# Two multiplications by one over the sums placed behind score steps, and GpSimd's weight residues computed in two halves

## The chip, the cores and the metric

One core of one Trainium2 chip runs the whole program as one launch. The metric is the device time of that launch in microseconds (us); the time before is the median of three runs. A profile of one further execution goes with it. Engines are named as in the profile: PE is TensorE (PEld its weight loads), DVE is VectorE, ACT is ScalarE, POOL is GpSimd, SP is the queue that issues most of the loads.

## The reference, cut to what matters

Two transformer-like blocks in float32 on a sequence of 1024 tokens of width 1024. The first block is gated linear attention with a short convolution and a feed-forward layer; the second is a spatial gating branch beside a dilated attention with 16 heads of 64. The part that the change touches is the dilated attention and every dense product with a weight matrix:

```python
s = einsum('bhrnqd,bhrnkd->bhrnqk', qb, kw) * Dh ** -0.5 - slopes * dist * dilation
p = exp(s - max(s)); l = sum(p)
o = einsum('bhrnqk,bhrnkd->bhrnqd', p, vw) / l
```

The kernel computes the three dilation patterns as one causal attention with a bias (distance times slope plus the logarithm of how many patterns hold the pair), which gives the same mixture.

## The kernel before, in words

**Dense products.** All weights are cut into 197 units of 1024 x 128. float32 accuracy is made from three reduced-precision products: high part of the weight by high part of the input, high by low, low by high (L791 to L793, and L974 to L976 in a part that works on sums of blocks). One unit is 16 groups of these three matmuls with 512 columns. For each unit SP loads the raw weights (`w_raw`, 128 x 1024), ACT copies them to the high part (`w_hi`, L1185), and POOL subtracts to get the low part, the residue (`w_lo`, L686). Two slots are used in turn. SP's next load into a slot waits for the residue's semaphore `w_lo` of that slot's unit, and PE's unit begins with a wait for `w_hi` and `w_lo`. The feed-forward and projection parts that use block sums have their own residue code (L721), in pieces of 128 x 512.

**Attention.** It runs under 32 further dense units: 8 pairs of heads, and for each pair four stages m = 0, 1, 2, 3 (head m // 2, token half m % 2). I call m = 0 and 2 early stages, m = 1 and 3 late stages. Into the 16 dense groups of a stage's unit PE weaves small steps, and each engine has a hand-written order of steps (`PE_STEPS`, `ACT_STEPS`, `DVE_STEPS`, one string for early and one for late stages). A stage works on its own scores and at the same time finishes the stage before it. The steps are:

- `s` on PE (L1094, L1095): a chunk of scores into PSUM (`aux`). Late stages have eight, s0 to s7, for four token blocks with two chunks each. s(n) waits until `r(n-2)` is done, because two PSUM banks alternate.
- `r` on DVE (L2215): adds the bias, keeps the row minimum, writes to the buffer of p (`att_p_late` or `att_p_early`); it is followed by a short read of the accumulator.
- `e` on ACT (L1595): the exponential of a token block with its row sum.
- `n` on DVE (L2225 and L2227, function `normed`): one over the row sum, then the multiplication of the block of p by it. In late stages the blocks are 640, 768, 896 and 1024 wide. PE's first transposition of the next stage waits for all four.
- `t` on PE (L1110): transposes p of the stage before; `p` on ACT (L1605): its high part; `l` on DVE (L2234, `p_lo`): its low part; `o` on PE (L1122, L1123): multiplies by v. `o(k)` waits for `l(k)`, and `t(k)` for `l(k-1)`.
- `z` on DVE (L2198) copies the unit's result out of PSUM; `w` on ACT is the high part of the next unit's weights, after which POOL makes the residue; `m` (L2250) finishes a gate and is there only in m = 1 (for the stage before, m - 1 = 0) and in m = 2; `b` (L2091), `q` (L2096), `k` (L2101) prepare the next head; `O` adds the two halves of the output; `v` splits v and is there only in m = 1.

In stage m = 1 POOL multiplies y by its gate first (L756), then makes the residue (L686), and after `m` multiplies another tile (L751). In m = 3 it has only the residue.

An engine works its own list strictly in order: whatever stands behind a waiting step waits as well.

Of the kernel before, what the change touches and what calls it, by code (L numbers as in the profile page):

```python
# [106 lines left out]
def group(q):  # L107

    return q - 6 if 6 <= q < 14 else None
# [61 lines left out]
def chunks_of(m):  # L171
# [25 lines left out]
]  # L197
DVE_STEPS = [
    "O l0 k l1 z l2 r0 l3 r1 n0 l4 r2 n1 l5 r3 n2 l6 m n3 l7",
    "v0 r0 v1 O r1 r2 z n0 l0 r3 r4 n1 l1 r5 m r6 r7 l2 n2 b l3 n3 q",  # L200
]

PE_REST = "t0 t1//o0 t2//o1 t3//o2 t4//o3 t5//o4 t6//o5 t7//o6//o7//".split("/")
# [26 lines left out]
def two_blocks(nc, xT, weights, vecs, gate_up, mix_w, mix_b, dist, logm, ident, out):  # L230
    f32, f32r = mybir.dt.float32, mybir.dt.float32r
    ALU = mybir.AluOpType
# [3 lines left out]
    with ctx:  # L236
# [4 lines left out]
        def place(name, cols, dt=f32, offset=None, rows=P):  # L241
            nonlocal top
            shape = [rows] + (list(cols) if isinstance(cols, (list, tuple)) else [cols])
            size = 4 * int(np.prod(shape[1:]))
            if offset is None:
                offset, top = top, top + (size + 63) // 64 * 64
            at[name] = offset
            return nc.alloc_sbuf_tensor_at(name, shape, dt, offset=offset)
# [6 lines left out]
        WR = place("w_raw", [2, KT, P])  # L255
        WH = place("w_hi", [2, KT, P], f32r)
        WL = place("w_lo", [2, KT, P], f32r)
# [83 lines left out]
        def sem(name):  # L341
            return ctx.enter_context(nc.semaphore(name))
# [5 lines left out]
        w_hi, w_lo, mm_done, evac = sem("w_hi"), sem("w_lo"), sem("mm_done"), sem("evac")  # L348
# [51 lines left out]
        def product(p, i, six, pair):  # L400

            return (six, 6 * p + i + 1) if i < 6 else (pair, units_before(p) + 2)
# [8 lines left out]
        def half(p, i):  # L411
            return (7 * own(p) + i + 2 + (min(p // 4, 3) if p < DUOS else min(own(p) // 8, 1))) % 4
# [15 lines left out]
        def quarter(p, i):  # L428

            if i in (0, 1, 3, 6):  # L430
                return WS[:, (0, 1, 3, 6).index(i)]
            row, col = {2: (0, 0), 4: (0, 1), 5: (1, 1)}[i]
            return w_pair(p)[:, row].rearrange("p (j e) c -> p e j c", e=2)[:, col]
# [23 lines left out]
        def all_stages(engine, stage):  # L457


            first, final = Pair(0), Pair(PAIRS - 1)  # L460
            stage(first, 0, head=False)
            stage(first, 1, before=(first, 0))
            with engine.Fori(0, PAIRS - 1) as j:
                now, following = Pair(0, j), Pair(1, j)
                stage(now, 2, before=(now, 1), done=(now, 0))
                stage(now, 3, before=(now, 2), done=(now, 1))
                stage(following, 0, before=(now, 3), done=(now, 2))
                stage(following, 1, before=(following, 0), done=(now, 3))
            stage(final, 2, before=(final, 1), done=(final, 0))
            stage(final, 3, before=(final, 2), done=(final, 1), head=False)  # L470
# [211 lines left out]
        @block.gpsimd  # L682
        def _(pool):
            def split(u):
                pool.wait_ge(w_hi, u.count(1))
                pool.tensor_tensor(WL[:, u.slot], WR[:, u.slot], WH[:, u.slot].bitcast(f32),  # L686
                                   ALU.subtract).then_inc(w_lo, 1)

            def splits(c, n):
                if n >= 2:  # L690
                    with pool.Fori(0, n // 2) as i:
                        split(Unit(c, i, 2))
                        split(Unit(c + 1, i, 2))
                if n % 2:
                    split(Unit(c + n - 1))

            pool.memset(ONES[:], 1.0).then_inc(consts, 1)
            for u in range(2, U_OUT + 2):
                split(Unit(u))
                if u == 3:  # L700
                    pool.wait_ge(rs, 1)
                    pool.memset(RESET, 1.0).then_inc(g_const, 1)
                    pool.wait_ge(g_const, 1)
                    pool.memset(RESET.rearrange("p (c t) -> p c t", t=CHUNK)[:, :, 0:1], 0.0).then_inc(g_const, 1)
                if u == 10:
                    pool.wait_ge(g_tp, 4)
                    for s in range(2):
                        pool.memset(SC[:, s], 0.0).then_inc(g_const, 1)
                if u - 2 in AT_SCORES:
                    for h in (2 * AT_SCORES.index(u - 2), 2 * AT_SCORES.index(u - 2) + 1):  # L710
                        pool.wait_ge(sc_cp, h + 1)
                        pool.affine_select(out=SC[:, h % 2], in_=SC[:, h % 2], compare_op=ALU.is_ge, fill=0.0,
                                           base=0, pattern=[[0, NBLK], [1, P]], channel_multiplier=-1
                                           ).then_inc(sc_sel, 1)
            splits(U_OUT + 2, U_DUO - U_OUT - 2)

            def lo_half(p, i):
                pool.wait_ge(*product(p, i, d_hi, w_hi))
                h = half(p, i)
                at4 = slice(4 * (h % 2), 4 * (h % 2) + 4)  # L720
                pool.tensor_tensor(WL[:, h // 2, at4], quarter(p, i), WH[:, h // 2, at4].bitcast(f32),  # L721
                                   ALU.subtract).then_inc(*((d_lo, 1) if i < 6 else (w_lo, 2)))

            for p in range(DUOS):
                for i in range(7):
                    lo_half(p, i)
            splits(U_DOWN, V_DUO - U_DOWN)

            def mask(g):
                pool.wait_ge(gat_in[g % 2], 32 * (g // 2 + 1))  # L730
                w3 = MIXES[:, g % 2, 0:1]
                pool.affine_select(out=w3, in_=w3, compare_op=ALU.is_ge, fill=0.0, base=0,
                                   pattern=[[0, 1], [1, P]], channel_multiplier=-1).then_inc(w_sel, 1)

            for q in range(V_DUOS):
                for i in range(7):
                    lo_half(DUOS + q, i)
                    if i == 2 and group(q) is not None:
                        mask(group(q))
            splits(U_ATT, 2)  # L740


            def stage(pair, m, before=None, done=None, head=True):
                if m == 1 and done:
                    gate_y(done[0])
                if before:
                    split(pair.unit(m).plus(1))
                if m == 1:
                    pool.wait_ge(gated, pair.count(2, 1))
                    pool.wait_ge(mx_in, pair.count(16, 16))  # L750
                    pool.tensor_tensor(MXL[:], MXL[:], AG[:], ALU.mult).then_inc(ya_up, 1)  # L751

            def gate_y(pair):
                pool.wait_ge(yh, pair.count(4, 4))
                pool.wait_ge(gated, pair.count(2, 2))
                pool.tensor_tensor(Y[:], Y[:], SBG[:], ALU.mult).then_inc(yb_up, 1)  # L756

            all_stages(pool, stage)
            split(Unit(U_PA + 1))
            gate_y(Pair(PAIRS - 1))  # L760
            splits(U_PA + 2, UNITS - U_PA - 2)
            for t in range(2):
                pool.wait_ge(rs, 6 + t)
                for k in ENDED_BY_ACT:
                    dst = XR[:, k, t * HALF:(t + 1) * HALF]
                    pool.tensor_tensor(dst, dst, R[:, t * HALF:(t + 1) * HALF], ALU.mult).then_inc(fin_pool, 1)
# [1656 lines left out]
```

## Time and profile before

| | us |
|---|---|
| median of three runs | 2412.66 |
| lowest and highest of the runs | 2410.06, 2413.32 |
| the profiled execution's own time | 2410.62 |
| its span in the profile | 2408.9 |
| PE busy | 2351.6 (98% of the span) |
| DVE busy | 1345.0 (56%) |
| ACT busy | 861.6 (36%) |
| POOL busy | 736.6 (31%) |

The mean granted clock of PE over the span is 0.994 of full speed. Spans on PE are modelled: a 512-column matmul is shown as 0.39 us long, while in an undisturbed stretch the next one starts 0.23 us after it. So what a wait costs is read from starts, not from ends. The attention lies between about 1523 and 2118 us of the span.

### The profile page before, as it was taken

How to read it: one execution, taken by the hardware profiler on the slowest of the kernel's cores; microseconds unless marked ns; L12 is line 12 of the kernel's file. 1: busy time of each engine (PE TensorE's matmuls, PEld its weight loads, DVE VectorE, ACT ScalarE, POOL GpSimd, SP SyncE). 2: the span in 40 equal slices, each digit the busy share in tenths (PEclk: the TensorE clock that was granted, in tenths of full speed). 3: DMA queues.
4: the chain of work that ended last, by engine and by line, in shares of the span. 5: the costliest groups of instructions: out<-in, count | busy, mean ns of one | idle time of the engine just before them, and what ended most of it. 6: DMA issues, size and time to landing. Idle time of an engine off the chain costs nothing.

```text
span 2408.9 us, 29740 instructions
## 1 busy us (share of the span) xinstructions
PE 2351.6 (98%) x11076; PEld 1938.9 (80%) x11076; DVE 1345.0 (56%) x1790; ACT 861.6 (36%) x1293; POOL 736.6 (31%) x416
## 2 busy tenths in 40 slices
PE   9999999999999999999999999999999999999997
PEld 6888788878888888888888888778787787778886
DVE  4444763754444443347653444777877778753444
ACT  4422222242333331143343223555545555441122
POOL 2121221264555522222455555211122112212221
PEclk9999999999999999999999999999999999999998
DMA  3111222232222243233312223523233232353223
GB/s 133 44 44 35 88 79 96 86 144 85 79 79 80 84 169 105 70 114 114 118 53 83 101 95 111 178 76 113 78 113 106 77 113 78 105 181 124 105 96 113
DMA packets 69168, 237.94 MB, mean 99 GB/s; under 512 B 8241, under 2 KB 10449, under 8 KB 68945
## 3 DMA queue, kind: packets, MB, share of 16 engines
q1 hardware_dynamic: 53568, 181.53, 22.2%
q10 hardware_dynamic: 15504, 55.10, 5.7%
q8 instruction: 65, 1.06, 0.2%
q14 instruction: 31, 0.25, 0.0%
HBM read 177.35 MB, written 59.24 MB: 98 GB/s over the span
## 4 chain that ended last, share of the span: by engine, by line
PE 93%; DVE 4%; issue 1%; DMA 1%; ACT 1%; SPq 0%; DVEq 0%; ACTq 0%
PE dense L791 18%; PE dense L792 18%; PE dense L793 18%; PE dense L974 9%; PE dense L975 9%; PE dense L976 9%; PE aux L1110 3%; PE aux L1094 2%; PE aux L1095 1%; PE aux L1123 1%; PE aux L1122 1%; PE aux L1057 1%; DVE att_p_lo L2234 1%; DVE x_lo L1964 1%; PE aux L821 0%
## 5 line engine op out<-in xcount | busy, mean ns | idle before, releaser
L686 POOL TENSOR_TENSOR w_lo<-w_raw,w_hi 128x1024 fp32r<-128x1024 f32 x123 | 303.3, 2466 | 1097.0 <-ACT w_hi L1185 1087.9
L791 PE MATMUL dense<-x_hi,w_hi 128*128 128x512 f32 x1456 | 596.7, 410 | 5.8 <-DVE x_lo L1736 2.1
L792 PE MATMUL dense<-x_lo,w_hi 128*128 128x512 f32 x1456 | 570.7, 392 | 0.0
L793 PE MATMUL dense<-x_hi,w_lo 128*128 128x512 f32 x1456 | 570.7, 392 | 0.0
L1185 ACT CAST w_hi<-w_raw 128x1024 fp32r<-128x1024 f32 x121 | 127.1, 1050 | 555.7 <-PE dense L793 548.8
L793 PEld LDWEIGHTS dense<-x_hi,w_lo 128*128 128x128 f32 x1456 | 274.8, 189 | 59.8
L791 PEld LDWEIGHTS dense<-x_hi,w_hi 128*128 128x128 f32 x1456 | 275.5, 189 | 56.6 <-issue 8.6
L792 PEld LDWEIGHTS dense<-x_lo,w_hi 128*128 128x128 f32 x1456 | 276.1, 190 | 46.6 <-issue 1.9
L721 POOL TENSOR_TENSOR w_lo<-w_sums,w_hi 128x512 fp32r<-128x512 f32 x144 | 228.3, 1594 | 240.9 <-ACT w_hi L1341 240.9
L974 PE MATMUL dense<-x_hi,w_hi 128*128 128x512 f32 x576 | 226.1, 392 | 0.0
L976 PE MATMUL dense<-x_hi,w_lo 128*128 128x512 f32 x576 | 224.2, 389 | 0.0
L975 PE MATMUL dense<-x_lo,w_hi 128*128 128x512 f32 x576 | 224.2, 389 | 0.0
L1341 ACT CAST w_hi<-w_sums 128x512 fp32r<-128x512 f32 x144 | 89.2, 620 | 242.8 <-DVE w_sums L1973 176.1
L974 PE MATMUL dense<-x_sums_split,w_hi 128*128 128x512 f32 x432 | 168.4, 390 | 2.4 <-DVE work L2180 1.2
L976 PE MATMUL dense<-x_sums_split,w_lo 128*128 128x512 f32 x432 | 168.2, 389 | 0.0
L975 PE MATMUL dense<-x_sums_split,w_hi 128*128 128x512 f32 x432 | 168.1, 389 | 0.0
L1605 ACT CAST att_p_hi<-aux 128x512 fp32r<-128x512 f32 x192 | 92.2, 480 | 145.9 <-PE aux L1110 145.5
L2234 DVE TENSOR_TENSOR att_p_lo<-aux,att_p_hi 128x512 fp32r<-128x512 f32 x192 | 106.3, 554 | 60.3 <-ACT att_p_hi L1605 58.0
L791 PE MATMUL dense<-work_split,w_hi 128*128 128x512 f32 x352 | 137.0, 389 | 1.5 <-DVE work L2049 1.5
L793 PE MATMUL dense<-work_split,w_lo 128*128 128x512 f32 x352 | 136.9, 389 | 0.0
L792 PE MATMUL dense<-work_split,w_hi 128*128 128x512 f32 x352 | 136.9, 389 | 0.0
L974 PEld LDWEIGHTS dense<-x_hi,w_hi 128*128 128x128 f32 x576 | 108.2, 188 | 23.0 <-issue 1.0
(270 smaller groups left out, 3815.7 us busy)
## 6 DMA issues: line engine op xcount, KB each, us to landing
w_raw<-weights SPq DMA_DIRECT2D x163, 512.0 KB, 4.1
w_raw_b<-weights SPq DMA_DIRECT2D x34, 512.0 KB, 4.3
kept_qkv<-work ACTq DMA_DIRECT2D x24, 512.0 KB, 2.7
kept_m<-work ACTq DMA_DIRECT2D x22, 512.0 KB, 2.6
work<-kept_m SPq DMA_DIRECT2D x22, 512.0 KB, 3.3
residual<-xT SPq DMA_DIRECT2D x16, 512.0 KB, 7.1
kept_x<-residual ACTq DMA_DIRECT2D x16, 512.0 KB, 2.6
att_q<-kept_qkv SPq DMA_DIRECT2D x32, 256.0 KB, 3.9
```

The costliest lines, as they stand in the source:

```text
L686: pool.tensor_tensor(WL[:, u.slot], WR[:, u.slot], WH[:, u.slot].bitcast(f32), ALU.subtract).then_inc(w_lo, 1)
L721: pool.tensor_tensor(WL[:, h // 2, at4], quarter(p, i), WH[:, h // 2, at4].bitcast(f32), ALU.subtract).then_inc(*((d_lo, 1) if i < 6 else ...
L791: pe.matmul(dst, WH[:, u.slot, k], hi, start=(k == 0), stop=False)
L792: pe.matmul(dst, WH[:, u.slot, k], lo, start=False, stop=False)
L793: last = pe.matmul(dst, WL[:, u.slot, k], hi, start=False, stop=(k == nk - 1))
L974: pe.matmul(bank(b), wh, hi[:, j], start=(first and j == 0), stop=False, skip_group_check=True)
L975: pe.matmul(bank(b), wh, lo[:, j], start=False, stop=False, skip_group_check=True)
L976: last = pe.matmul(bank(b), wl, hi[:, j], start=False, stop=(j == 3), skip_group_check=True)
L1185: act.copy(WH[:, u.slot], WR[:, u.slot]).then_inc(w_hi, 1)
L1341: act.copy(WH[:, h // 2, 4 * (h % 2):4 * (h % 2) + 4], quarter(p, i)).then_inc(*((d_hi, 1) if i < 6 else (w_hi, 2)))
L1605: act.copy(PH[:, k % 2, lo:HALF], PA[:, bank, lo:HALF]).then_inc(ph, 1)
L2234: dve.tensor_tensor(PL[:, k % 2, lo:HALF], PA[:, bank, lo:HALF], PH[:, k % 2, lo:HALF].bitcast(f32), ALU.subtract).then_inc(pl, 1)
```

## The change

In late stages the multiplication of the first block, n0, moves from behind `z` to behind `r4`, so that `l0`, `r3` and `r4` come before it. The second, n1, moves from behind `r4` to behind `r5`, so that `l1` and `r5` come before it. Early stages stay as they are. The residue of a unit is made by two POOL instructions of 128 x 512 in place of one of 128 x 1024; the semaphore is incremented by the second one alone. That holds for every unit whose residue `split` makes, throughout the kernel, 123 by the profile.

```diff
 DVE_STEPS = [
     "O l0 k l1 z l2 r0 l3 r1 n0 l4 r2 n1 l5 r3 n2 l6 m n3 l7",
-    "v0 r0 v1 O r1 r2 z n0 l0 r3 r4 n1 l1 r5 m r6 r7 l2 n2 b l3 n3 q",
+    "v0 r0 v1 O r1 r2 z l0 r3 r4 n0 l1 r5 n1 m r6 r7 l2 n2 b l3 n3 q",
 ]
...
             def split(u):
                 pool.wait_ge(w_hi, u.count(1))
-                pool.tensor_tensor(WL[:, u.slot], WR[:, u.slot], WH[:, u.slot].bitcast(f32),
-                                   ALU.subtract).then_inc(w_lo, 1)
+                for at4 in (slice(0, 4), slice(4, 8)):
+                    last = pool.tensor_tensor(WL[:, u.slot, at4], WR[:, u.slot, at4],
+                                              WH[:, u.slot, at4].bitcast(f32), ALU.subtract)
+                last.then_inc(w_lo, 1)
```

## Rows read from the trace of the kernel before

**Rows 1.** Who waited for whom on PE, all of the span: total, times, longest (us)
```profile
PE aux L1094 <- DVE softmax_stats L2215: 25.1, 16, 1.9
PE aux L938 <- ACT work L1287: 3.3, 1, 3.3
```
**Rows 2.** PE in order of time, stages m = 1 (1696) and m = 3 (1733): start, length
```profile
1693.92 0.39 PE L793 MATMUL dense<-x_hi,w_lo 128*128 128x512 f32 x1
1696.22 0.45 PE L1094 MATMUL aux<-att_k_hi,att_q_split 128*128 128x384 f32 x1 [1.91 <-DVE softmax_stats L2215]
1696.50 0.34 PE L1095 MATMUL aux<-att_k_lo,att_q_split 128*128 128x384 f32 x1
1696.68 0.40 PE L1122 MATMUL aux<-att_p_hi,att_v_split 128*128 128x512 f32 x1
...
1733.21 0.44 PE L1094 MATMUL aux<-att_k_hi,att_q_split 128*128 128x384 f32 x1 [1.24 <-DVE softmax_stats L2215]
```
**Rows 3.** DVE in order of time in the stage m = 1 at 1696
```profile
1692.37 0.15 DVE L2225 RECIPROCAL softmax_stats<-softmax_stats 128x1 f32<-128x1 f32 x1
1692.56 2.61 DVE L2227 TENSOR_SCALAR att_p_late<-att_p_late,softmax_stats 128x640 f32<-128x640 f32 x1
1695.09 0.68 DVE L2234 TENSOR_TENSOR att_p_lo<-aux,att_p_hi 128x512 fp32r<-128x512 f32 x1
1695.69 0.47 DVE L2215 CUSTOM_DVE_ANT_0 att_p_late<-aux,att_bias,softmax_stats 128x256 f32<-128x256 f32 x1
...
1697.46 0.62 DVE L2227 TENSOR_SCALAR att_p_late<-att_p_late,softmax_stats 128x768 f32<-128x768 f32 x1
...
1704.59 0.28 DVE L2234 TENSOR_TENSOR att_p_lo<-aux,att_p_hi 128x128 fp32r<-128x128 f32 x1
```
**Rows 4.** ACT and POOL in order of time in the same stage
```profile
1692.22 0.59 ACT L1605 CAST att_p_hi<-aux 128x512 fp32r<-128x512 f32 x1
1697.69 0.48 ACT L1605 CAST att_p_hi<-aux 128x384 fp32r<-128x384 f32 x1 [0.46 <-PE aux L1110]
1692.42 2.39 POOL L686 TENSOR_TENSOR w_lo<-w_raw,w_hi 128x1024 fp32r<-128x1024 f32 x1
```
**Rows 5.** POOL and DVE in order of time in an early stage, m = 2
```profile
1635.20 2.40 POOL L686 TENSOR_TENSOR w_lo<-w_raw,w_hi 128x1024 fp32r<-128x1024 f32 x1 [7.54 <-ACT w_hi L1185]
...
1636.59 0.68 DVE L2234 TENSOR_TENSOR att_p_lo<-aux,att_p_hi 128x512 fp32r<-128x512 f32 x1
```
**Rows 6.** Waits from 1523 to 2118 (one row), then PE's timeline in the stage m = 1
```profile
PEld aux L1122 <- DVE att_p_lo L2234: 2.0, 6, 0.4
...
1704.60 0.40 PE L793 MATMUL dense<-x_hi,w_lo 128*128 128x512 f32 x1
1704.93 0.33 PE L1122 MATMUL aux<-att_p_hi,att_v_split 128*128 128x128 f32 x1
...
1705.60 0.49 PE L791 MATMUL dense<-x_hi,w_hi 128*128 128x512 f32 x1 [0.23 <-issue]
```
**Rows 7.** Busy time by window (after POOL: granted clock, DMA share, GB/s), then PE's timeline
```profile
1620.40:1624.40 4.00, 4.00 (x13) 3.27 (x14) 2.85 (x8) 2.83 (x5) 0.00 (x0) 0.58 0.00 0
...
1620.36 0.44 PE L1094 MATMUL aux<-att_k_hi,att_q_split 128*128 128x384 f32 x1 [1.91 <-DVE softmax_stats L2215]
1658.32 0.44 PE L1094 MATMUL aux<-att_k_hi,att_q_split 128*128 128x384 f32 x1 [1.24 <-DVE softmax_stats L2215]
```
**Rows 8.** Groups by line and shape on POOL (busy us, mean ns), then one row of its timeline
```profile
L686 POOL TENSOR_TENSOR w_lo<-w_raw,w_hi 128x1024 fp32r<-128x1024 f32 x123 | 303.3, 2466 | 1097.0 <-ACT w_hi L1185 1087.9 <-ACT w_hi L1582 4.5 <-ACT w_hi L1421 4.5
...
512.31 1.29 POOL L721 TENSOR_TENSOR w_lo<-w_raw_b,w_hi 128x512 fp32r<-128x512 f32 x1
```
**Rows 9.** DVE in order of time in the convolution, before the wait at L938
```profile
282.45 3.28 DVE L1906 TENSOR_TENSOR work<-work,rstd 128x1024 f32<-128x1024 f32 x1
```
**Rows 10.** POOL and PE in order of time where the first attention unit begins
```profile
1518.32 2.58 POOL L686 TENSOR_TENSOR w_lo<-w_raw,w_hi 128x1024 fp32r<-128x1024 f32 x1 [4.53 <-ACT w_hi L1582]
...
1522.72 0.47 PE L791 MATMUL dense<-x_hi,w_hi 128*128 128x512 f32 x1 [0.62 <-DVE work L2180]
```

## The prediction

> **What bounds the kernel now.** The table has PE busy for 98% of the span, so PE's stream sets the end and only its waits can be won. I read the waits of PE first: the largest by far is that of the score matmul for DVE's running minimum, 25.1 us in 16 times; the next is 3.3 us, once [rows 1]. There are 16 late stages, so it is one wait in each. PE's timeline shows where: at the 384-column chunk, which is s5, 1.91 us in a stage m = 1 and 1.24 us in a stage m = 3 [rows 2]; 8 x 1.91 + 8 x 1.24 = 25.2 us. s5 waits for r3.
>
> DVE's timeline shows why r3 is late. n0's multiplication, of 640 columns, takes 2.61 us, while n1's, of 768, takes 0.62 us [rows 3]. POOL's residue runs from 1692.42 to 1694.81 [rows 4], and n0 ends 0.36 us behind its end: n0 stood still beside POOL and then ran in some 0.56 us. l0 and r3 stood behind it on DVE. The high part that l0 needs was there at 1692.81 [rows 4].
>
> **What a wait costs in PE's stream.** Undisturbed, a 512-column matmul is followed by the next after 0.23 us, so s5 would have started at 1693.92 + 0.23 = 1694.15; it started at 1696.22, 2.07 us late [rows 2]. Its successor comes after 0.28 us where the next step takes 0.18 us [rows 2], 0.10 us more. So m = 1 loses 2.17 us, and m = 3, by the same 0.26 us on top of the wait, 1.50 us.
>
> **Part 1, n0 behind r4.** From 1692.37, where n0's reciprocal began, DVE now waits for the high part and runs l0 from 1692.84 (0.68 us; successive DVE rows overlap by 0.08 us), then r3 from 1693.44 to about 1693.95 with the reading of its minimum [rows 3, 4]. s5 wants to start at 1694.15 and its weight load some 0.2 us earlier, so r3 is there at the last moment; in m = 3 it has 0.7 us to spare by the shorter wait (1.91 - 1.24). I count no wait at s5 and keep 0.3 us per stage m = 1 for the range. n0 then starts near 1694.7 and meets the end of POOL's second half at most; its cost lies in DVE's idle time before l1, which waits for PE's t1 and ACT's copy.
>
> **Part 2, n1 behind r5.** Before, n1 ended at 1698.08 and the high part for l1 came at 1698.17 [rows 3, 4]: n1 was in the shadow of that wait. Now it stands behind l1 and r5, with 0.15 + 0.62 us and the gap between, less one overlap, about 0.74 us, on DVE's path from t1 to the end of the stage. s6 and s7 are not reached by it, since r4 and r5 are done before. What is late next is l3. The wait of o3's weight load for l3 is there already, 6 times, 2.0 us together [rows 6]. By starts: o3 would have begun at 1704.60 + 0.23 = 1704.83 and began at 1704.93, and the dense matmul behind its two short ones came at 1705.60 [rows 6] where some 0.17 us after o3 are usual: 0.6 us lost. So in a stage m = 1 l3 sets the time of everything behind it. Before, l3 ended 1704.87 - 1698.17 = 6.70 us behind the copy that l1 waits for [rows 3, 4]; that copy comes 2.17 us earlier, the chain is 0.74 us longer, and the stage wins 2.17 - 0.74 = **1.43 us**, with a wait of l3's of about 1.1 us in its place at o3. In m = 3 there is neither `m` nor POOL's second multiplication in DVE's chain, and no such wait is in the trace; n1's 0.74 us goes into that slack and the whole **1.50 us** is won.
>
> **The clock.** In two of the eight stages m = 1 the granted clock fell behind the wait; the window 1620.40 to 1624.40 has a mean of 0.58 [rows 7], so most of it passed at 1.2 GHz, not 2.4. The price: from one restart of s5 to the next is 1658.32 - 1620.36 = 37.96 us with the fall [rows 7] and 1733.21 - 1696.22 = 36.99 us without [rows 2], 0.97 us. No stage m = 3, with 1.24 us of waiting, had one. With waits of about 1 us or less I take both away: **1.9 us**.
>
> **Part 3, the residue in halves.** POOL's instruction of 1024 columns takes 2.39 us alone, one of 512 takes 1.29 us [rows 4, 8]: 0.19 us more for each of the 123, 23 us on an engine that is busy for 31%. The group's idle time before its instructions, 1097.0 us [rows 8], is the cover. Behind POOL wait PE's next unit and SP's load. The tightest place that I looked at is the first attention unit: the residue ends at 1520.90 and PE starts at 1522.72 [rows 10], 1.8 us of slack. So 0 us. Can the halves win anything by themselves? In attention hardly, as n0 has been moved out of their way. Elsewhere a DVE instruction caught by POOL could go in between; the one case on PE's path is L1906, 3.28 us [rows 9], longer than a whole residue of 2.39 us [rows 4] and so mostly waiting. But its successors, too, work on buffers outside PSUM and would meet the second half. Bounds: +0.5 us (the second dispatch) and -1.3 us (one half less to wait for); I take 0, since POOL's time in DVE's way stays the same.
>
> **The sum.** 8 x 1.43 + 8 x 1.50 + 1.9 + 0 = 11.4 + 12.0 + 1.9 = 25.3 us. Against the profiled execution's own 2410.62 us this is 2385.3. That execution lies 2.0 us below the median of the runs, 2412.66, and the forecast is for the median: **2387.4 us**.
>
> **A rule on GpSimd and VectorE.** l0 and r3 now run while POOL makes the residue, so it matters whether they stand still as n0 did. In the early stage, where l2 fell wholly within POOL's 1635.20 to 1637.60, it took its usual 0.68 us [rows 5]; its input comes from PSUM and one SBUF buffer, as with r3. The Trainium skill, GPSIMD Engine Reference, section Key points, says that GpSimd contends with DVE instructions that run in a two-port mode or have two SBUF inputs. By that rule neither l0 nor r3 is held, and n0 and the successors of L1906 are. The trace agrees for l with 0.68 us, and no row shows a 256-column r3 beside POOL. What it would be if they were held is the second rival.
>
> **The rivals.**
> 1. *n1 finds room* (12%). If l3 were not the bound of m = 1, because the n2, `b` and l3 part shortens once POOL's multiplication falls elsewhere, each such stage would win 2.17 us and the 0.6 us at o3 in the six stages too: 8 x 2.17 + 12.0 + 1.9 + 3.6 = 34.9 us at most; with the wait at o3 unchanged 31.3 us, **2381.4 us**. Against it: n2, `b` and l3 all follow r7, which follows n1 and `m`.
> 2. *l0 and r3 are held as well*, each until POOL is done (4%): r3 would end as late as before, both moves win nothing, **2412 us**, no change. Against it speaks the 0.68 us [rows 5].
> 3. *l0 becomes the wait* (16%). DVE has nothing to do before the high part comes, and r3 and r4 queue behind l0. That part is made by ACT behind the copy of the next weights. Were it 0.5 us later than in this trace in all m = 1 stages, s5 would wait for 0.5 us or more with a restart, some 0.6 us each: 25.3 - 4.8 = 20.5; were it 1.2 us, 8 x (2.17 - 1.3 - 0.74) + 12.0 + 1.9 = 15 us, **2397.7 us**. For it: r3 is ready at the last moment as it is.
> 4. *The residue is late* (2%), the one that ends slower. POOL's two halves let DVE in between; if the residue then ended past the start of its unit, PE would wait in every unit. It decides once 1.8 us is used up [rows 10]. By 0.19 us, plus one DVE operation as long as a half, 1.29 us [rows 8], it comes to 1.5 us, so the place would hold; a further operation in between would break it, and at a loss of 0.8 us in each of 123 units the time would be 2387.4 + 98 = **2486 us**.
> 5. *The change doesn't do what it says* hardly applies: both edits are read off the code. The smallest version, in which a late r5 at s7 or another unseen wait eats half of the gain (6%), is 2400 us.
>
> **How the numbers follow.** The forecast has 60%, the rivals 12, 4, 16, 2 and 6%. The range reaches from rival 1 to rival 3, 2380.5 to 2397.5 us, which leaves out rivals 2, 4, 5 and the far end of 3. About 0.2%, 4.8 us, is what a measurement of this kernel can tell from no change, so faster means under 2407.8 us: the forecast and rivals 1, 3 and 5, 94%; the same 4%; slower 2%.
>
> **What the changed profile would show.** The row L1094 waiting for L2215, 25.1 us, is gone or below 3 us. The 640-column multiplication takes 0.56 to 0.9 us in place of 2.61 us. The weight load at L1122 waits for L2234 in all eight stages m = 1, for about 1 us each. POOL has twice the instructions at L686, of about 1.29 us, and its busy time rises by some 23 us. From s5 of an m = 1 stage to s5 of the next m = 3 stage it is still about 36.3 to 37 us without a fall of the clock, and the attention as a whole is 25 us shorter. I would be wrong if s5 still waits for 1 us or more in m = 1, if the wait at o3 stays at 0.4 us, or if PE waits for POOL anywhere.

## The result and the profile after

| | before | after |
|---|---|---|
| median, us | 2412.99 (4 runs) | 2385.43 (4 runs) |
| lowest and highest, us | 2410.06, 2414.69 | 2382.76, 2388.25 |
| the profiled execution's own time, us | 2410.62 | 2388.25 |
| its span, us | 2408.9 | 2386.5 |

The ratio of the times is 0.9887 (95% interval 0.987 to 0.9904), so the kernel is 27.6 us faster by the medians. The forecast was 2387.4 us with a range of 2380.5 to 2397.5. In the changed kernel all line numbers behind the edit are two higher and those of `split` one: the scores are L1096 and L1097, the transpositions L1112, `o` L1124 and L1125, `r` L2217, `n` L2227 and L2229, `l` L2236, the dense matmuls L793 to L795, the residue L687.

The busy times of the whole profiled execution, then the group of the residue:

```profile
PE 2350.5 (98%) x11076; PEld 1939.1 (81%) x11076; DVE 1284.5 (54%) x1790; ACT 860.8 (36%) x1293; POOL 800.7 (34%) x539
...
L687 POOL TENSOR_TENSOR w_lo<-w_raw,w_hi 128x512 fp32r<-128x512 f32 x246 | 367.7, 1516 | 1029.2 <-ACT w_hi L1187 1020.2
```

PE is the bound as before. DVE is busy 60.5 us less and POOL 64.1 us more. The waits on PE of the changed kernel, the two largest:

```profile
PE aux L1124 <- DVE att_p_lo L2236: 3.8, 8, 0.5
PE aux L940 <- ACT work L1289: 3.1, 1, 3.1
```

The row that stood first [rows 1], the scores waiting for `r3` 16 times, has no counterpart. In its place `o3` waits for `l3`, once in each of the eight stages m = 1. The wait in the convolution went from 3.3 to 3.1 us. Now the stage m = 1 that answers to [rows 2 to 4]. DVE in order of time:

```profile
1688.22 0.69 DVE L2236 TENSOR_TENSOR att_p_lo<-aux,att_p_hi 128x512 fp32r<-128x512 f32 x1 [0.38 <-ACT att_p_hi L1607]
1688.83 0.47 DVE L2217 CUSTOM_DVE_ANT_0 att_p_late<-aux,att_bias,softmax_stats 128x256 f32<-128x256 f32 x1
...
1690.04 0.68 DVE L2229 TENSOR_SCALAR att_p_late<-att_p_late,softmax_stats 128x640 f32<-128x640 f32 x1
1691.39 0.56 DVE L2236 TENSOR_TENSOR att_p_lo<-aux,att_p_hi 128x384 fp32r<-128x384 f32 x1 [0.67 <-ACT att_p_hi L1607]
...
1692.59 0.62 DVE L2229 TENSOR_SCALAR att_p_late<-att_p_late,softmax_stats 128x768 f32<-128x768 f32 x1
...
1698.53 0.28 DVE L2236 TENSOR_TENSOR att_p_lo<-aux,att_p_hi 128x128 fp32r<-128x128 f32 x1
```

ACT and POOL in the same stage:

```profile
1690.88 0.48 ACT L1607 CAST att_p_hi<-aux 128x384 fp32r<-128x384 f32 x1 [0.50 <-PE aux L1112]
...
1687.82 2.55 POOL L687 TENSOR_TENSOR w_lo<-w_raw,w_hi 128x512 fp32r<-128x512 f32 x2
```

PE in the same stage, at s5 and at o3:

```profile
1689.31 0.39 PE L795 MATMUL dense<-x_hi,w_lo 128*128 128x512 f32 x1
1689.54 0.34 PE L1096 MATMUL aux<-att_k_hi,att_q_split 128*128 128x384 f32 x1
...
1697.99 0.40 PE L795 MATMUL dense<-x_hi,w_lo 128*128 128x512 f32 x1
1698.86 0.33 PE L1124 MATMUL aux<-att_p_hi,att_v_split 128*128 128x128 f32 x1 [0.47 <-DVE att_p_lo L2236]
1699.02 0.28 PE L1125 MATMUL aux<-att_p_lo,att_v_split 128*128 128x128 f32 x1
1699.53 0.49 PE L793 MATMUL dense<-x_hi,w_hi 128*128 128x512 f32 x1 [0.23 <-issue]
```

**Read them in this order.** `l0` and `r3` ran inside POOL's 1687.82 to 1690.37 at 0.69 and 0.47 us, as long as before, so they were not held. (The 2.55 us are both halves of the residue, merged into one row.) s5 started 0.23 us behind the dense matmul before it: no wait is left. n0 began at 1690.04, 0.33 us ahead of POOL's end, and took 0.68 us in place of 2.61 [rows 3]. Then the price: n1, now behind `r5`, lies between the copy that `l1` waits for (end 1691.36) and `l3` (end 1698.81), 7.45 us in place of 6.70. o3 would have begun at 1697.99 + 0.23 = 1698.22 and began at 1698.86, and the dense matmul behind it followed after 0.67 us where some 0.17 us are usual. So PE lost 0.64 + 0.50 = 1.14 us at o3, of which the row of waits names 0.47.

**Where the time came from.** The starts of the 384-column score matmuls give it without any modelled end. The first of them is s2 of the first early stage, the last is s5 of the last stage m = 3; between them lie 2108.25 - 1529.62 = 578.63 us before and 2085.01 - 1531.72 = 553.29 us after: **25.3 us** are won inside the attention. From s5 of m = 3 to s5 of the next m = 1 it is 35.72 us after and 37.89 before (2.17 less, the term of s5 in m = 1). From s5 of m = 1 to s5 of m = 3 it is 36.19 after and 36.99 before where the clock did not fall. That is 0.80 less, where the forecast's 1.50 - 0.74 is 0.76. Together 2.97 us for each pair of stages. Outside these two points the spans are 1830.3 and 1833.2 us, so nothing was won there. Over half of the 2.9 us came near 1105 us, where the granted clock was low for longer. The window 1104 to 1114, before and after (the columns as in [rows 7]):

```profile
1104.00:1114.00 10.00, 10.00 (x42) 7.69 (x42) 3.39 (x8) 1.64 (x4) 0.00 (x0) 0.83 0.01 2
1104.00:1114.00 10.00, 10.00 (x43) 8.78 (x43) 3.55 (x9) 1.59 (x3) 0.00 (x0) 0.66 0.01 2
```

This is not the work of the change: one and the same kernel, n0_moved_whole below, has 0.66 there in one execution and 0.83 in another.

The granted clock behind s5 of two stages m = 1 of the changed kernel (the columns as in [rows 7]); the other six stages m = 1 show 1.00 as well:

```profile
1617.63:1621.63 4.00, 4.00 (x21) 3.34 (x20) 3.26 (x10) 3.31 (x6) 0.72 (x1) 1.00 0.00 0
1689.54:1693.54 4.00, 4.00 (x21) 3.37 (x21) 3.26 (x10) 3.30 (x6) 0.83 (x1) 1.00 0.00 0
```

The two falls of before [rows 7] are gone: in the attention the engine stays at 2.4 GHz.

### The profile page after: what moved, and what is told of

The parts are those of the page before. It is cut to its first block, busy times and chain, and to the rows that moved or that the text cites. A ratio compares the mean times of both kernels' runs of the same rounds, so it can differ in the third digit from the quotient of the medians.

```text
span 2386.5 us, 29863 instructions
## 1 busy us (share of the span) xinstructions
PE 2350.5 (98%) x11076; PEld 1939.1 (81%) x11076; DVE 1284.5 (54%) x1790; ACT 860.8 (36%) x1293; POOL 800.7 (34%) x539
## 4 chain that ended last, share of the span: by engine, by line
PE 92%; DVE 4%; issue 2%; ACT 1%; DMA 1%; DVEq 0%; SPq 0%; ACTq 0%
PE dense L793 18%; PE dense L794 18%; PE dense L795 18%; PE dense L976 9%; PE dense L977 9%; PE dense L978 9%; PE aux L1112 2%; PE aux L1125 1%; PE aux L1124 1%; PE aux L1097 1%; PE aux L1096 1%; PE aux L1059 1%; DVE x_lo L1966 1%; PE aux L823 0%; DVE att_p_late L2217 0%
## 5 line engine op out<-in xcount | busy, mean ns | idle before, releaser
L687 POOL TENSOR_TENSOR w_lo<-w_raw,w_hi 128x512 fp32r<-128x512 f32 x246 | 367.7, 1516 | 1029.2 <-ACT w_hi L1187 1020.2
L793 PE MATMUL dense<-x_hi,w_hi 128*128 128x512 f32 x1456 | 595.7, 409 | 4.8 <-DVE x_lo L1738 2.8
L795 PE MATMUL dense<-x_hi,w_lo 128*128 128x512 f32 x1456 | 570.2, 392 | 0.0
L795 PEld LDWEIGHTS dense<-x_hi,w_lo 128*128 128x128 f32 x1456 | 274.1, 188 | 59.6
L793 PEld LDWEIGHTS dense<-x_hi,w_hi 128*128 128x128 f32 x1456 | 275.0, 189 | 56.0 <-issue 7.5
L2236 DVE TENSOR_TENSOR att_p_lo<-aux,att_p_hi 128x512 fp32r<-128x512 f32 x192 | 106.5, 555 | 71.4 <-ACT att_p_hi L1607 71.0
L793 PE MATMUL dense<-work_split,w_hi 128*128 128x512 f32 x352 | 137.0, 389 | 2.1 <-DVE work L2051 2.1
L795 PE MATMUL dense<-work_split,w_lo 128*128 128x512 f32 x352 | 136.9, 389 | 0.0
L1939 DVE TENSOR_TENSOR residual<-dense,residual 128x1024 f32<-128x1024 f32 x32 | 39.2, 1225 | 170.6 <-PE dense L795 170.6
```

Source lines behind the costliest of these rows:

```text
L687: last = pool.tensor_tensor(WL[:, u.slot, at4], WR[:, u.slot, at4], WH[:, u.slot, at4].bitcast(f32), ALU.subtract)
L793: pe.matmul(dst, WH[:, u.slot, k], hi, start=(k == 0), stop=False)
L795: last = pe.matmul(dst, WL[:, u.slot, k], hi, start=False, stop=(k == nk - 1))
L2236: dve.tensor_tensor(PL[:, k % 2, lo:HALF], PA[:, bank, lo:HALF], PH[:, k % 2, lo:HALF].bitcast(f32), ALU.subtract).then_inc(pl, 1)
```

## The experiments

My theory was that of the forecast: n0 caught by POOL made `r3` late, the order alone cures it, the halves do nothing, and n1's new place costs 0.7 us for each m = 1. The rivals were that the halves bring the gain, or part of it outside the attention, and that n1's move is needed or free. All variants differ from the kernel before in the string for late stages, in `split`, or in both. "Pair" is the time from s5 of one m = 1 to that of the next, for a pair without a fall of the clock that is neither the first nor the last (such pairs of one kernel agree within about 0.1 us), "attention" is the stretch defined above; "gain" is against the median of the kernel before in the same batch of runs.

| kernel | late string, from `z` | residue | median | ratio (95%) | gain | pair | attention |
|---|---|---|---|---|---|---|---|
| before | z n0 l0 r3 r4 n1 l1 r5 m | whole | 2412.99 | 1 | | 74.88 | 578.63 |
| changed | z l0 r3 r4 n0 l1 r5 n1 m | halves | 2385.43 | 0.9887 (0.987 to 0.9904) | 27.6 | 71.91 | 553.29 |
| order_only | as changed | whole | 2388.60 | 0.9904 (0.9889 to 0.992) | 22.6 | 71.95 | 553.39 |
| halves_only | as before | halves | 2392.32 | 0.992 (0.9907 to 0.9934) | 18.9 | 72.66 | 558.35 |
| quarters_only | as before | quarters | 2391.65 | 0.9911 (0.9895 to 0.9928) | 20.8 | 72.25 | 555.84 |
| n1_moved_whole | z n0 l0 r3 r4 l1 r5 n1 m | whole | 2417.72 | 1.0024 (1.0014 to 1.0034) | -6.5 | 75.58 | 583.77 |
| n0_moved | z l0 r3 r4 n0 n1 l1 r5 m | halves | 2382.15 | 0.9882 (0.9867 to 0.9897) | 29.1 | 71.20 | 547.34 |
| n0_moved_whole | as n0_moved | whole | 2382.50 | 0.9875 (0.9858 to 0.9891) | 30.0 | 71.22 | 547.52 |

**The order alone.** Edit, on the kernel before:

```diff
-    "v0 r0 v1 O r1 r2 z n0 l0 r3 r4 n1 l1 r5 m r6 r7 l2 n2 b l3 n3 q",
+    "v0 r0 v1 O r1 r2 z l0 r3 r4 n0 l1 r5 n1 m r6 r7 l2 n2 b l3 n3 q",
```

> Only the new order of DVE steps, residues of units whole as before. Theory: the order brings all of the gain. From the restart of s5 in one m = 1 stage to the next it is 71.9 us as in the changed kernel (74.9 before), the 640-column multiplication takes under 0.8 us, the matmul at o3 waits about 0.5 us for l3 eight times, and the time is that of the changed kernel within 2 us, 2384 to 2387 us. Rival: the halves bring a share of it; then this kernel is slower than the changed one by 3 us or more, and n0 still takes over 1.5 us.

It gave 2388.60 us. Its largest wait on PE in the attention:

```profile
PE aux L1122 <- DVE att_p_lo L2234: 3.8, 8, 0.5
```

Its group of n0's multiplication (busy us, mean ns, idle before):

```profile
L2227 DVE TENSOR_SCALAR att_p_late<-att_p_late,softmax_stats 128x640 f32<-128x640 f32 x16 | 8.9, 553 | 0.6
```

The waits, the pair and the attention (553.39 against 553.29 us) are those of the changed kernel. The whole gain of the attention is the order's. n0 takes 553 ns, which is its length without POOL beside it. The median lies 1.6 us above the expected range and 3.2 us above the changed kernel's, which by itself is what the rival asked for. But n0 takes 0.55 us and not 1.5, the trace puts only 0.7 us of it outside the attention (1833.9 against 1833.2 us), and the changed kernel measured again, below, gave 2387.41 us. So I put the 3.2 us down mostly to the spread between batches.

**The halves alone.** Edit, on the kernel before:

```diff
-                pool.tensor_tensor(WL[:, u.slot], WR[:, u.slot], WH[:, u.slot].bitcast(f32),
-                                   ALU.subtract).then_inc(w_lo, 1)
+                for at4 in (slice(0, 4), slice(4, 8)):
+                    last = pool.tensor_tensor(WL[:, u.slot, at4], WR[:, u.slot, at4],
+                                              WH[:, u.slot, at4].bitcast(f32), ALU.subtract)
+                last.then_inc(w_lo, 1)
```

> Only the residues in halves, DVE's order as before. Theory: DVE's n0 stands still until POOL's running instruction ends, so it waits for the first half alone and goes in between the two: its multiplication takes about 1.5 us in m = 1 and 0.8 us in m = 3 instead of 2.61 and 1.94; s5 waits about 0.8 us in m = 1 and 0.1 to 0.4 us in m = 3; gain 8 x 1.1 + 8 x 1.0, with the two falls of the clock 18 us, so 2393 to 2397 us. Rival (n0 is held until the whole residue is done, halves or not): 2.6 us stays, the time is that of before.

It gave 2392.32 us: the halves alone bring 18.9 us. Its remaining wait on PE for DVE's `r3`:

```profile
PE aux L1096 <- DVE softmax_stats L2217: 5.7, 7, 0.8
```

Its group of n0's multiplication:

```profile
L2229 DVE TENSOR_SCALAR att_p_late<-att_p_late,softmax_stats 128x640 f32<-128x640 f32 x16 | 18.1, 1129 | 0.6
```

n0 on DVE and the residue on POOL in order of time, in one stage m = 1:

```profile
1689.38 1.51 DVE L2229 TENSOR_SCALAR att_p_late<-att_p_late,softmax_stats 128x640 f32<-128x640 f32 x1
...
1689.25 2.77 POOL L687 TENSOR_TENSOR w_lo<-w_raw,w_hi 128x512 fp32r<-128x512 f32 x2
```

n0 began 0.13 us behind POOL's first piece and ended at 1690.89, while POOL worked until 1692.02. So n0 is let through between the pieces: it stands still for one piece and not for the whole residue. In m = 3, where it begins 0.81 us into the piece and not 0.13 us, it takes 0.83 us. s5 of m = 1 is left with a wait of 0.81 us. s5 of m = 3 stands in no row of waits, but it starts at 1727.81, 0.52 us behind the dense matmul before it, so it is 0.29 us late. The forecasts for n0 and for both waits came true; the time is 0.7 us below the expected 2393 to 2397 us. The two edits work on the same wait, so their gains (22.6 and 18.9 us) do not add up. With the new order the halves find nothing left to cure in the attention.

**Four pieces.** Edit, on the kernel before:

```diff
-                pool.tensor_tensor(WL[:, u.slot], WR[:, u.slot], WH[:, u.slot].bitcast(f32),
-                                   ALU.subtract).then_inc(w_lo, 1)
+                for at4 in (slice(0, 2), slice(2, 4), slice(4, 6), slice(6, 8)):
+                    last = pool.tensor_tensor(WL[:, u.slot, at4], WR[:, u.slot, at4],
+                                              WH[:, u.slot, at4].bitcast(f32), ALU.subtract)
+                last.then_inc(w_lo, 1)
```

> DVE's order as before, residues in four pieces of 256 columns. Theory: n0 stands still to the end of whichever piece runs: about 0.9 us in both kinds of late stage instead of 2.61 and 1.94 (whole) and 1.13 on the mean (halves); the wait at s5 falls to 0.3 us or less in m = 1 and disappears in m = 3; period 72.0 us or less, total about 2389 us. Rival (the hold is a fixed time or a share of bandwidth, not to the end of the instruction): n0 takes 1.1 us or more as with the halves. POOL's busy time at these lines rises to 123 x (4 x 0.7 us) = 340 us or more.

It gave 2391.65 us, 2.7 us above the expected 2389. Its wait on PE for DVE's `r3`:

```profile
PE aux L1096 <- DVE softmax_stats L2217: 4.3, 16, 0.3
```

Its group of n0's multiplication:

```profile
L2229 DVE TENSOR_SCALAR att_p_late<-att_p_late,softmax_stats 128x640 f32<-128x640 f32 x16 | 15.5, 971 | 0.6
```

Against the halves n0 lost only another 158 ns on the mean, and s5 still waits 0.3 us in all 16 late stages. That the wait disappears in m = 3 was expected and did not happen: there n0 takes 0.98 us, more than the 0.83 us with halves, because a new piece has begun only 0.11 us before it. The three traces settle what holds n0. In all 48 late stages of before, halves_only and quarters_only it ends 0.35 us (once 0.36) behind the end of the POOL instruction during which it began, whether that one took 2.40, 1.29 or 0.74 us. As it takes 0.55 us alone, it must have got going some 0.2 us ahead of that recorded end; why is open.

POOL is busy for 897.6 us in place of 803.7, and this reaches PE. At the first attention unit the four pieces take 6.02 us where the whole residue took 2.58 [rows 10]. POOL, then PE, with quarters:

```profile
1521.93 6.02 POOL L687 TENSOR_TENSOR w_lo<-w_raw,w_hi 128x256 fp32r<-128x256 f32 x4 [4.53 <-ACT w_hi L1584]
...
1528.05 0.47 PE L793 MATMUL dense<-x_hi,w_hi 128*128 128x512 f32 x1 [2.34 <-issue]
```

PE begins the unit 0.10 us behind POOL's end, 2.50 us late, so the residue fits as its releaser although the row names none. This is the mechanism of rival 4, in one unit. Finer pieces shorten the standstill of n0 less and less and cost more elsewhere; putting n0 elsewhere ends it.

**n1 alone.** Edit, on the kernel before:

```diff
-    "v0 r0 v1 O r1 r2 z n0 l0 r3 r4 n1 l1 r5 m r6 r7 l2 n2 b l3 n3 q",
+    "v0 r0 v1 O r1 r2 z n0 l0 r3 r4 l1 r5 n1 m r6 r7 l2 n2 b l3 n3 q",
```

> The kernel before with n1 alone moved behind r5, residues whole. Theory: s5 waits as before, 25 us in 16 times, and n1 adds 0.74 us to the chain to l3 in m = 1, where no slack is left: the wait at o3 grows from 0.1 to 0.5 us or more, and the kernel is slower than before by 4 to 6 us, about 2418 us. Rival (moving n1 costs nothing): 2413 us, o3 waits 0.1 us.

It gave 2417.72 us, 6.5 us slower than the kernel before. Its waits on PE, the two of the attention that matter:

```profile
PE aux L1094 <- DVE softmax_stats L2215: 24.5, 16, 1.9
PE aux L1122 <- DVE att_p_lo L2234: 1.9, 4, 0.5
```

The clock behind s5 by windows (the columns as in [rows 7]), in a stage that kept it and in two that did not:

```profile
1622.20:1626.20 4.00, 4.00 (x19) 3.37 (x20) 2.56 (x8) 3.36 (x5) 0.00 (x0) 1.00 0.00 0
1697.83:1701.83 4.00, 4.00 (x14) 3.28 (x15) 2.35 (x8) 3.15 (x5) 0.00 (x0) 0.63 0.00 0
1773.71:1777.71 4.00, 4.00 (x13) 3.30 (x14) 1.72 (x6) 2.49 (x5) 0.00 (x0) 0.57 0.00 0
```

The wait at s5 stays, the stretch from s5 of m = 1 to s5 of m = 3 grows from 36.99 to 37.70 us where the clock did not fall, 0.71 us, and o3 waits longer: n1 in its new place is a pure cost, near the 0.74 us of the forecast; the 6.5 us are 0.5 us more than the 4 to 6 expected. Seven stages m = 1 had a wait of 1.9 us here; four of them show a fall.

**n0 alone, with and without the halves.** Edit of the first, on the changed kernel; the second has the same string and the whole residue:

```diff
-    "v0 r0 v1 O r1 r2 z l0 r3 r4 n0 l1 r5 n1 m r6 r7 l2 n2 b l3 n3 q",
+    "v0 r0 v1 O r1 r2 z l0 r3 r4 n0 n1 l1 r5 m r6 r7 l2 n2 b l3 n3 q",
```

> The changed kernel, but n1 stands directly behind n0, ahead of l1 and r5, in the shadow of DVE's wait for l1's input. Theory: n1's 0.74 us leaves the chain to l3, the wait at o3 goes from 0.48 us back to 0.1 us or less, 0.6 to 0.7 us less in each m = 1 stage, 71.2 us from one m = 1 stage to the next, and 5 us less than the changed kernel: 2379 to 2382 us. Rival (the wait at o3 comes from POOL's longer residue or from the 1.4 to 2.2 us by which PE is now early, not from n1): it stays at 0.4 to 0.5 us and so does the time, 2385 us.

> n0 behind r4, n1 directly behind n0, residues whole as before. Theory: with n0 out of POOL's way the halves bring nothing more in attention, so this is the kernel with n0 moved and halves again: 71.2 us from one m = 1 stage to the next, total 2381 to 2384 us. Rival (a whole residue still holds n0 or n1 in m = 1, whose reciprocal starts about 0.1 us before the residue ends): the 640-column multiplication takes 0.8 us or more and l3 is late again, 71.5 to 71.9 us, 2385 us.

They gave 2382.15 and 2382.50 us, at the edge of the first expected range and inside the second, and neither rival came. With the whole residue, the wait of o3's weight load:

```profile
PEld aux L1122 <- DVE att_p_lo L2234: 2.8, 9, 0.4
```

PE in order of time at o3 of a stage m = 1:

```profile
1697.46 0.40 PE L793 MATMUL dense<-x_hi,w_lo 128*128 128x512 f32 x1
1697.78 0.33 PE L1122 MATMUL aux<-att_p_hi,att_v_split 128*128 128x128 f32 x1
1697.94 0.27 PE L1123 MATMUL aux<-att_p_lo,att_v_split 128*128 128x128 f32 x1
1698.45 0.49 PE L791 MATMUL dense<-x_hi,w_hi 128*128 128x512 f32 x1 [0.23 <-issue]
```

n1 lies here in the shadow of the wait for the copy that `l1` needs, as before the change, and o3 begins 0.09 us late in place of 0.64. The pair is 71.22 us against 71.95 with n1 behind `r5`, 8 x 0.73 = 5.8 us over the attention, and 553.39 - 547.52 = 5.9 us were measured. Of the 0.73 us, 0.55 lie at o3. The other 0.18 lie at o2, which with n1 behind `r5` starts 0.08 us later and costs another 0.10 us behind it. It is the fastest of the versions tried, with or without the halves.

**The two again, on the same chip.** No edit; the changed kernel and n0_moved_whole were run a second time side by side, because 3 to 6 us lay between them in different batches.

> The changed kernel once more, beside the next two on one chip. Theory: 71.9 us from one m = 1 stage to the next, 2385 to 2387 us.

> n0 behind r4, n1 directly behind n0, residues whole, once more. Theory: 71.2 us per pair and 3 to 6 us faster than the changed kernel, as n1 costs 0.7 us eight times on the path to l3; with whole residues nothing is lost. Rival (the difference seen before was between chips or runs): within 1 us of the changed kernel.

They gave 2387.41 us (2386.39 to 2388.19; ratio 0.9901, 0.9885 to 0.9918) and 2381.36 us (2380.09 to 2384.05; ratio 0.9879, 0.9862 to 0.9895), 6.1 us apart and no run of the one among those of the other, with attentions of 553.19 and 547.43 us. The changed kernel stands at 2385.4 and 2387.4 in two batches, with gains of 27.6 and 25.1 us.

**Can l3 be put ahead?** `l3` still bounds m = 1, behind n2 and `b`. Three variants move it. Edits, on n0_moved_whole: the first is n0_l3_first (and, with halves, n0_l3_first_halves), the second l3_n3_first:

```diff
-    "v0 r0 v1 O r1 r2 z l0 r3 r4 n0 n1 l1 r5 m r6 r7 l2 n2 b l3 n3 q",
+    "v0 r0 v1 O r1 r2 z l0 r3 r4 n0 n1 l1 r5 m r6 r7 l2 n2 l3 b n3 q",
```

```diff
-    "v0 r0 v1 O r1 r2 z l0 r3 r4 n0 n1 l1 r5 m r6 r7 l2 n2 b l3 n3 q",
+    "v0 r0 v1 O r1 r2 z l0 r3 r4 n0 n1 l1 r5 m r6 r7 l2 n2 l3 n3 b q",
```

> The same, and l3 stands ahead of b (the next head's bias) in late stages. Theory: what is left at o3 in m = 1 (0.1 us of waiting and 0.4 to 0.5 us of restart) is DVE's b in front of l3; with l3 first it goes and 0.6 us per m = 1 stage is won: 70.6 us from one m = 1 stage to the next, total 2376 to 2379 us. Rival (l3 waits for its input from ACT, or b is now late for r0 of the next stage, or n3 for t0): the period stays at 71.2 us or a wait appears at L1094 or L1110 in early stages.

It gave 2387.86 us (ratio 0.9899, 0.9882 to 0.9915) against the expected 2376 to 2379, 5.4 us slower than without the move. Its largest wait on PE:

```profile
PE aux L1110 <- DVE att_p_late L2227: 6.3, 15, 0.4
```

PE in order of time at the end of a stage m = 1:

```profile
1697.67 0.22 PE L1122 MATMUL aux<-att_p_hi,att_v_split 128*128 128x128 f32 x1
1697.73 0.28 PE L1123 MATMUL aux<-att_p_lo,att_v_split 128*128 128x128 f32 x1
1697.84 0.49 PE L791 MATMUL dense<-x_hi,w_hi 128*128 128x512 f32 x1
...
1699.17 0.66 PE L1110 MATMUL aux<-identity,att_p_late 128*128 128x128 f32 x4 [0.38 <-DVE att_p_late L2227]
```

o3 is cured (the dense matmul 0.17 us behind it), but `b` no longer fills DVE's time while it waits for ACT's copy, so n3 is later, and the first transposition of the next stage waits for it after 15 of the 16 late stages. That is the rival's n3.

> The same with residues in halves. Theory: equal to the one with whole residues in attention, 70.6 us, and 0.1 us more at the first unit, where PE comes to wait for the residue; total 2376 to 2380 us. Rival (the halves win outside attention, where DVE's instructions on two buffers outside PSUM are held less): 2 us or more faster than with whole residues.

It gave 2387.20 us (ratio 0.9894, 0.9878 to 0.9911), the same wait of 6.3 us and the same pair, 71.89 us. The attention is 552.9 us in both. So the halves bring nothing here that the time can tell from its spread, and the rival's 2 us did not come.

> The same, but late stages end l2 n2 l3 n3 b q: l3 and n3 both ahead of b. Theory from the run with l3 alone ahead of b, where t0 of the next stage came to wait 0.43 us for n3: n3 now ends 1.3 us earlier and that wait goes; o3 does not wait either; 70.6 to 71.0 us per pair, 2377 to 2380 us. Rival (b, q and the next stage's l0 end later by what DVE now idles for l3's input, 0.5 us in m = 1 and 1.1 us in m = 3, and o0 of the early stage waits for l0): a new wait at L1122 in early stages, 71.2 us or more, no gain.

It gave 2383.36 us (ratio 0.9885, 0.9869 to 0.9902), not the expected 2377 to 2380. Now the stretch from s5 of m = 1 to s5 of m = 3 is 35.22 us, 0.28 less than the best, but that from m = 3 to the next m = 1 is 36.22, 0.50 more. The wait that did it, one of seven:

```profile
1736.78 0.49 PE L1122 MATMUL aux<-att_p_hi,att_v_split 128*128 128x512 f32 x1 [0.24 <-DVE att_p_lo L2234]
```

It is o0 of the early stage m = 2: `b`, now the last but one step of its stage, pushes `O` and `l0` of the next one back. The pair is 71.44 us, between the two others. The form that would keep each half where it wins, `l3` and n3 ahead of `b` in m = 1 alone, was not tried.

## Why the prediction was right

- **What bounds the kernel, and why s5 waits.** Right. Moving n0 alone takes all 16 waits away (n0_moved_whole), and shortening the POOL instruction shortens n0 (2.61, 1.51 us in m = 1) without any change of order (halves_only). One detail of the reading does not add up: n0 ended 0.36 us behind POOL, which leaves no room for the 0.56 us that it was said to run after the standstill.
- **Part 1.** Right: the term of 2.17 us for m = 1 shows as 37.89 - 35.72 = 2.17 us. `l0` and `r3` ran beside POOL at full pace and s5 did not wait, so rivals 2 and 3 did not come, and no other wait ate the gain as in rival 5. I kept 0.3 us a stage for a late `r3`; it was not needed.
- **Part 2.** Right in mechanism and size: 0.74 us on DVE's path was forecast, 7.45 - 6.70 = 0.75 measured there, 0.71 us of the stretch to m = 3 by n1_moved_whole and 0.73 us of the pair by n0_moved_whole and order_only. Rival 1, that n1 finds room, is refuted. The "wait of about 1.1 us" was badly put: PE loses 1.14 us at o3 (and some 0.2 us at o2, which I had left out), but the records of waits call only 0.47 us of it a wait, so my sign that it must not "stay at 0.4 us" would have read this correctly forecast loss as a miss. It is read from starts.
- **The stretch from s5 of m = 1 to that of m = 3.** "About 36.3 to 37 us" did not follow from my own terms, which give 36.99 - 1.50 + 0.74 = 36.23; measured were 36.19 to 36.30 in the regular stages.
- **The clock.** Two falls disappeared, as put. Every fall inside the attention in these traces stood behind a wait of s5 of 1.9 us, two of eight before and four of seven in n1_moved_whole, and none behind one of 1.25 us or less. The price of a fall varies more than I took: in n1_moved_whole three stretches with one are 37.94, 37.99 and 38.57 us against 37.70, 0.2 to 0.9 us more.
- **Part 3.** The effect on the time was right in this order of steps (0 us: 553.29 against 553.39 us of attention), but two statements behind it were wrong. "POOL's time in DVE's way stays the same" is false: DVE is busy 1317.1 - 1284.5 = 32.6 us less with halves in the same order, and POOL, for which I forecast 23 us more, is busy 800.7 - 736.6 = 64.1 us more. A piece has a mean of 1516 ns where it takes 1.29 us alone [rows 8]; the pieces stand still in their turn. Of the 246 halves, 112 had no DVE step of over 0.25 us beside them that reads only buffers outside PSUM; these took 1.26 to 1.31 us. All 57 halves of more than 1.44 us had one. The multiplication of the convolution [rows 9] shows it in one place. DVE, then POOL, in the changed kernel:

```profile
282.81 2.20 DVE L1908 TENSOR_TENSOR work<-work,rstd 128x1024 f32<-128x1024 f32 x1
...
282.66 3.50 POOL L687 TENSOR_TENSOR w_lo<-w_raw,w_hi 128x512 fp32r<-128x512 f32 x2 [10.11 <-ACT w_hi L1187]
```

  DVE's step is 1.08 us shorter than its 3.28 us, and POOL's two pieces take 3.50 us in place of one of 2.39. PE's wait there fell by 0.2 us only, within the bounds that I had put on it.
- **The tightest place for the residue.** Wrong twice. First, the 1.8 us of slack at the first attention unit were used up. I had counted on a residue 1.5 us longer at most and a place that holds. POOL, then PE, there in the changed kernel:

```profile
1521.02 3.71 POOL L687 TENSOR_TENSOR w_lo<-w_raw,w_hi 128x512 fp32r<-128x512 f32 x2 [4.52 <-ACT w_hi L1584]
...
1524.83 0.47 PE L793 MATMUL dense<-x_hi,w_hi 128*128 128x512 f32 x1
```

  The residue took 1.13 us more than before. DVE, let in between the halves, finished the step that PE had waited for before so much earlier that PE's lateness at this unit fell from 0.78 to 0.18 us; now it starts 0.10 us behind POOL's end. The halves win 0.6 us here, and the same two values stand in every kernel with halves and every kernel with whole residues.

  Second, the very first split unit of the kernel is tighter. POOL and PE there, first before:

```profile
28.42 2.75 POOL L686 TENSOR_TENSOR w_lo<-w_raw,w_hi 128x1024 fp32r<-128x1024 f32 x1 [27.40 <-ACT w_hi L1185]
...
31.27 0.47 PE L791 MATMUL dense<-x_hi,w_hi 128*128 128x512 f32 x1 [1.93 <-DVE work L1795]
```

  and in the changed kernel:

```profile
28.68 2.93 POOL L687 TENSOR_TENSOR w_lo<-w_raw,w_hi 128x512 fp32r<-128x512 f32 x2 [27.67 <-ACT w_hi L1187]
...
31.71 0.47 PE L793 MATMUL dense<-x_hi,w_hi 128*128 128x512 f32 x1 [0.51 <-issue]
```

  In both PE starts 0.10 us behind POOL's end, so POOL's end fits as its releaser in both. The row of before names DVE's copy, but in the changed kernel PE starts while that copy (L1797, 31.24 to 32.46) still runs; the traces of halves_only and n0_moved name POOL's w_lo outright. By the sign that I had set, PE waiting for POOL anywhere, the forecast failed in both places. The lateness is 0.18 us at either and nothing like the 0.8 us a unit of rival 4.
- **The sum.** 25.3 us were forecast and 25.3 us were won in the attention. Its parts fit as well: the waits of s5 in m = 1 brought 17.2 us (8 x 2.17 = 17.4 by the forecast) and the eight stretches from there to m = 3 brought 8.1 us, the two falls among them (8 x 0.76 + 1.9 = 8.0). That the total agrees to the tenth is some luck: the medians gave 27.6 us, and 25.1 in the second batch, and the time outside the attention varied between 1830.3 and 1833.9 us over the traces of before, changed and order_only, as much as any term that is left.

The Trainium skill, SBUF — State Buffer, section SBUF: two separate sides, says that VectorE and GpSimd share a pair of ports as an exclusive lock: a GpSimd instruction, or a VectorE one in a two-port mode or with two SBUF inputs, holds it for its whole length if it starts first, and the other is blocked fully. The trace agrees for n0: begun second, it ends 0.35 us behind the end of the POOL instruction, whole [rows 3, 4] or a piece, and the POOL piece behind it lengthens from 1.29 to about 1.53 us once DVE gets its turn between them. n0 has one tensor input, so by that page it is held only in a two-port mode; no trace here shows an instruction's mode.

A finer cut so moves standstill from DVE to POOL. Of the 64.1 us more on POOL, 23 are the second instruction of each unit and the other 41 stand against the 32.6 us less on DVE.

## What to carry to other kernels

A DVE step that stands still beside a GpSimd instruction is best moved to where GpSimd is idle or where DVE would wait anyway; cutting the GpSimd instruction shortens the standstill only to one piece (n0 takes 2.27, 1.13 and 0.97 us on the mean with whole, halves and quarters, 0.55 alone) and gives the time to GpSimd, whose result can then be late. A step that is moved should land ahead of a wait that exists already: n0 behind `r4` did, n1 behind `r5` left such a place and cost 0.7 us a stage. When a change has several parts, try each alone: here one edit carries the whole gain, one is redundant beside it, and one costs some 5 us.

## What the runs showed that I had not expected

- A 128-column matmul that is 0.09 us late already costs PE 0.50 us behind it, as much as one that is 0.64 us late: the next dense matmul comes 0.67 us after o3 in both, and 0.17 us after it when o3 is in time (n0_l3_first). That is so in the six inner stages m = 1 (0.67 to 0.74 us); in the first and the last of the attention it comes 0.39 and 0.34 us after a late o3. At the 384-column s5 the same effect was 0.10 us. What makes it is open. Most of such a loss is in no row of waits.
- The lengthening of the halves is uneven: the mean is 1516 ns, but most take 1.29 us, and the 57 of 246 above 1.44 us carry nearly all of it, the longest with 3.34 us.
- An engine that is far from busy can still be late in one unit: POOL at 34% had 1.8 us of slack at the first attention unit, halves used it up and quarters made PE 2.50 us late there. No row of waits names POOL for it.
